# Reordering TensorE's first adaLN products and five late adaLN units in a two-layer convolution and attention trunk with mixture-of-experts

## The reference

```
m = silu(cvec) @ ada_w[i] + ada_b[i]          # (2 vectors) x 1024 x 6144, for each layer
h = rms_norm(x, g) * (1 + scale) + shift      # before the mixer and before the experts
y = y + gate * mixer(h);   y = y + gate2 * moe(h2)
q, k = rms_norm(q), rms_norm(k)               # layer 1; rotated for latent tokens
p = softmax([q @ k_local, q @ k_cached, sink])   # latent tokens; context tokens: own keys and sink
y_mixer = (p @ v) @ wo
```

## Time and profile before

| | us |
|---|---|
| median of three runs | 1288.72 |
| the profiled execution's own time | 1287.76 |
| its span, first to last instruction | 1285.9 |
| TensorE busy (share of span) | 1257.0 (98%) |
| VectorE busy | 442.9 (34%) |
| ScalarE busy | 327.5 (25%) |
| DMA, mean rate over the span | 387 GB/s |
| mean granted TensorE clock, share of full | 0.997 |

### The profile page before, as it was taken

One profiled execution on the slowest core, in us unless ns is written; L12 is line 12 of the kernel. 1 busy time (PEld: TensorE's weight loads), 2 busy tenths in 40 slices (PEclk: granted clock), 3 DMA queues, 4 the chain that ended last, 5 costly groups with the idle time before them and its releaser, 6 DMA issues.

```text
span 1285.9 us, 18888 instructions
## 1 busy us (share of the span) xinstructions
PE 1257.0 (98%) x6956; PEld 699.1 (54%) x6956; DVE 442.9 (34%) x1503; ACT 327.5 (25%) x728; POOL 62.3 (5%) x94
## 2 busy tenths in 40 slices
PE   7999999999999999999999899999999999999998
PEld 5776775544554455445454478554454445444544
DVE  3696372222222222222234727322222222222222
ACT  2486321221122112111131523222112212221211
POOL 0395000000000000000000000000000000000000
PEclk9999999999999999999999999999999999999999
DMA  9988999999999999999998786799999999999994
GB/s 331 382 335 365 406 395 397 417 419 419 421 421 419 420 421 421 421 420 420 392 382 346 173 359 229 304 407 419 419 420 421 421 420 421 421 420 420 420 418 194
DMA packets 87303, 497.43 MB, mean 387 GB/s; under 512 B 10889, under 2 KB 19761, under 8 KB 31952
## 3 DMA queue, kind: packets, MB, share of 16 engines
q1 hardware_dynamic: 86672, 496.47, 95.5%
q10 hardware_dynamic: 576, 0.22, 0.1%
HBM read 493.26 MB, written 3.41 MB: 386 GB/s over the span
## 4 chain that ended last, share of the span: by engine, by line
PE 86%; DVE 6%; DMA 4%; ACT 2%; issue 1%; POOL 0%; ACTq 0%; SPq 0%; DVEq 0%
PE ps L1024 33%; PE ps L1056 17%; PE ps L1067 9%; PE ps L995 7%; PE ps L661 4%; DMA S<-in_exp_w_up_dram 3%; DVE ps L1729 3%; PE ps L789 3%; PE ps L938 2%; PE ps L629 2%; PE ps L1042 1%; PE ps L979 1%; DMA W<-in_norm_ffn_dram 1%; PE ps L1034 1%; PE ps L649 1%
## 5 line engine op out<-in xcount | busy, mean ns | idle before, releaser
L1024 PE MATMUL ps<-ring,xg 128*64 128x512 f32 x1344 | 296.4, 593 | 0.2
L1024 PEld LDWEIGHTS ps<-ring,xg 128*64 128x64 f32 x1344 | 101.6, 137 | 189.4 <-issue 175.0
L1024 PE MATMUL ps<-S,xg 128*64 128x512 f32 x704 | 154.9, 592 | 1.2 <-DMA S<-in_exp_w_up_dram 1.2
L1056 PE MATMUL ps<-ring,W 128*64 128x512 f32 x672 | 153.5, 598 | 0.0
L2025 DVE TENSOR_TENSOR ypart<-ps,ypart 128x512 fp32r<-128x512 f32 x128 | 88.6, 692 | 179.8 <-ACT ypart L1514 179.8
L2014 DVE SCALAR_TENSOR_TENSOR vec<-silu_h,W,ps 128x256 f32<-128x256 f32 x64 | 30.8, 482 | 333.7 <-ACT silu_h L1508 333.6
L1067 PEld LDWEIGHTS ps<-comb,ypart 128*128 128x128 f32 x1024 | 126.3, 190 | 18.6 <-issue 18.6
L1067 PE MATMUL ps<-comb,ypart 128*128 128x256 f32 x1024 | 135.2, 285 | 0.0
L1508 ACT ACTIVATE silu_h<-ps 128x256 f32<-128x256 f32 x64 | 24.7, 386 | 408.2 <-PE ps L1024 408.2
L1503 ACT ACTIVATE xg<-ps 128x384 f32<-128x384 f32 x176 | 83.3, 492 | 168.0 <-PE ps L995 168.0
L1514 ACT ACTIVATE ypart<-ps 128x512 fp32r<-128x512 f32 x128 | 76.5, 597 | 184.6 <-PE ps L1056 184.6
(11 more groups left out here) (265 smaller groups left out, 1141.2 us busy)
## 6 DMA issues: line engine op xcount, KB each, us to landing
ring<-in_exp_w_gate_dram SPq DMA_DIRECT2D x86, 1024.0 KB, 16.1
ring<-in_exp_w_up_dram SPq DMA_DIRECT2D x86, 1024.0 KB, 19.4
ring<-in_exp_w_down_dram SPq DMA_DIRECT2D x86, 1024.0 KB, 19.2
S<-in_exp_w_gate_dram SPq DMA_DIRECT2D x44, 1024.0 KB, 16.8
S<-in_exp_w_up_dram SPq DMA_DIRECT2D x44, 1024.0 KB, 20.2
S<-in_exp_w_down_dram SPq DMA_DIRECT2D x44, 1024.0 KB, 19.3
ring<-in_ada_w_dram SPq DMA_DIRECT2D x24, 1024.0 KB, 20.5
S<-in_ada_w_dram SPq DMA_DIRECT2D x16, 1024.0 KB, 15.1
```

Of the source, the lines that this page charges most:

```text
L1024: mm = pe.matmul(PGU[64 * b:64 * b + 64, :].rearrange("p (h f) -> p h f", h=2), xg[:, places[k][m], 64 * b:64 * b + 64], gate_up_of(w[b])[ ...
L1056: mm = pe.matmul(bank[64 * b:64 * b + 64, :], hidT[:, j, 64 * b:64 * b + 64], down_of(w[b])[:, j, n * 512:(n + 1) * 512], start=(j == 0), ...
```

## The change: the order on TensorE, at two places

No other engine's list changes. The number of products that nobody reads rises by twelve; everything else is moved.

```diff
@@ front, in _(pe)
             pe.wait_ge(cond_ready, 1)
             sum_squares(1, 7)
+            keep_clock(ps[2], 20)
+            ada_half_products(0, 0)
             pe.wait_ge(ld_rows, 128)
             ... the ten transposes of the small rows
-            keep_clock(ps[2], 8)
-            for i in range(4):
+            for i in range(1, 4):
                 ada_half_products(0, i)
@@ heads of layer 1, in _(pe)
                     ada_products([EARLY + 10], ps[7])
                     at_values(0)
 
+                    ada_products([EARLY + 11], ps[7])
                     at_transposes(2)
                     at_scores(2)
-                    ada_products([EARLY + 11], ps[7])
                     at_transposes(3)
+                    ada_products([EARLY + 12], ps[7])
                     at_values(1)
 
                     at_transposes(4)
-                    ada_products([EARLY + 12], ps[7])
+                    ada_products([EARLY + 13], ps[7])
                     at_scores(3)
                     at_transposes(5)
-                    ada_products([EARLY + 13], ps[7])
+                    ada_products([EARLY + 14], ps[7])
                     at_values(2)
 
-                    ada_products([EARLY + 14], ps[7])
+                    ada_products([EARLY + 15], ps[7])
                     at_transposes(6)
-                    ada_products([EARLY + 15], ps[7])
                     at_transposes(7)
                     at_values(3)
```

## The result

The changed kernel takes 1290.85 us against 1287.42 us (medians of nine runs each, side by side): ratio 1.0028, interval 1.002 to 1.0037. It is 3.4 us slower. The forecast was +0.1, 1288.8 in all, and the range ended at 1290.8. (The three runs on which the forecast stands had a median of 1288.72, 1.3 us above that of the nine.) The profiled execution has a span of 1289.0 against 1285.9, +3.1 us, and the losses of this one execution can be read from it one by one.

A forecast was written before the change was run, and what follows sets the result against it. TensorE was taken as the bound, with the front waiting for unit 7's load and the heads for VectorE. Front 0.0, heads +0.1 and expert loads 0.0 gave +0.1 us, 1288.8 us; range 1286.5 to 1290.8.

The forecast's parts named there:

- The front's bound: Front: the last pair waits for unit 7's load at 24.2 us, so the new order gains nothing; term 0.0.
- Rival A: Front not bound by unit 7's landing: pair 3 at 21.8 instead of 25.2, -3.4 us; chance 0.07.
- the 3.7 us: Front: by the skill's clock rule, the stretch without its waits for loads would end 3.7 us earlier.
- The heads' order: Heads: filled waits come back as longer ones at `at_transposes(3)` and `at_transposes(7)`; term +0.1 us, bounds -0.2 and +0.4.
- the load of expert 0: Heads: the load would start at 726.7 instead of 730.56 us; term 0.0.
- Rival B: Heads pass on the filled waits before `at_transposes(2)` and `at_values(1)`: -1.8 us, 1287.0; chance 0.07.
- The clock: Front: two waits of 1.4 and 1.8 us replace one of 4.55; a clock fall at 24.3 would cost +1.3 to +5.0.
- rival C: Front: clock falls between 20 and 24.3 us, slowing the work behind: +1.3 to +5.0, 1290.1 to 1293.8; chance 0.13.
- C's long case: Front: half clock lasts through the first convolution chunk from 28.28, +5.0 us in all; chance 0.03.
- 1.9 us to spare: Front: the wait for unit 7 hides the twelve added products, which would otherwise cost 2.8 us.
- The page's rule: TensorE: a long pause between bursts of matmuls returns it to half rate; the trace agreed for the 4.55 us pause.

The follow-up runs named there:

- the repeat: The changed kernel measured again beside the kernel of before: 1290.57 against 1287.45 us, ratio 1.0025.
- heads part alone: Only the second half of the diff, the heads, applied to the kernel of before: 1289.88 against 1287.67 us, ratio 1.0015.
- the filler: Heads half of the diff on the kernel of before, plus 6 unread products ahead of the last head's transposes: 1287.55 against 1287.40 us, ratio 1.0002.
- front part alone: Only the first half of the diff, the front, applied to the kernel of before: 1288.28 against 1287.67 us, ratio 1.0006.
- its filler: Changed kernel plus 5 and 7 unread products in the front's two waits for loads: 1290.15 us against 1287.67 for before, ratio 1.0021.
- the kernel with both waits filled: Changed kernel plus 4 and 6 unread products in the front and 6 ahead of the last head's transposes: 1288.83 us against 1287.45 for before, ratio 1.0013.
- front part with eight products: Front half of the diff on the kernel of before, with 8 unread products instead of 20: 1288.48 against 1287.40 us, ratio 1.001.

## Why the prediction was wrong

- **The front's bound was right.** Pair 3 starts at 24.21 because unit 7 lands then, whatever TensorE did before; the waits were forecast at 1.4 and 1.8 us and measured at 1.30 and 1.64. Rival A is dead. One figure beside it, the 3.7 us by which the stretch without its waits would end earlier, has no working: rival A's own sum gives 3.4, and nothing else hangs on it.
- **The heads' order was right.** +0.1 forecast, +0.14 in the profile, and +0.15 in time once the wait is filled. The waits that are filled do come back one step later, and the load of expert 0 starts at 728.70, which less the 2.0 us is the 726.7 that was forecast. Rival B is dead.
- **The step that failed is "The clock".** It gave rival C 0.13 because "neither pause is nearly as long as the 4.55 us one", and it looked at the front alone. Pauses of 1.2 to 1.6 us were enough in three of five profiles with that front unfilled (once behind both, twice at the first), in the one place where the last pair and the transposes have no slack: +1.2 to +1.5, the size that C gave. The term for the heads was priced as a chain of engines, with the longer wait of 1.6 us "of idle time ahead of it in place of 0.57" written down and its clock not asked for. That was the larger loss: 1.3 and 0.35 in the profile, 3.0 in that of the repeat, +2.2 in the medians of the part alone. C's long case (half rate through the first chunk) did not occur in any profile, but its like did in the heads of the repeat.
- **A term was missing:** "1.9 us to spare" hides the twelve products' time but not their length in the list of instructions. They moved a fetch in front of the landing of a load that had 0.4 us of slack, 100 us later: +0.8 in the profile. How much of it reaches the medians is not shown.
- **The page's rule.** The Trainium skill ("TensorE: Matmul & The Clock Gate", section "Why this matters for your kernels") warns of a long pause. Here the clock fell at waits of 1.31, 1.54, 1.57 and 1.60 us, the first of them behind 7.5 us of work without a break, and in other executions it did not fall at such waits; the measurement decides. So the 4.55 us pause of before, which the prediction took as the measure, was no measure: with 1.54 us in its place the fall was the same.
- **The cost is not fixed.** My range treated the clock as one event, there or not. The same kernel took 1287.3 at a mean clock of 1.0 and 1293.4 at 0.993; the median depends on how often the falls come. The chance of C was too low: 0.13 for a fall that came in three of five profiles in the front alone.
- **What stays open:** the parts alone add up to 2.8 us (0.6 and 2.2) of the 3.1 to 3.4; that the clock is the cause is shown for the heads by the filler, and for the front by profiles only, since neither the front part (+0.6) nor its filler is clear of noise in the medians.

## What to carry to other kernels

Work that fills a wait does two things: it spends the time, and it keeps the matrix engine's clock up for what stands behind the wait. Before moving such work, list every wait that gets longer and ask what runs right behind it; a move that only exchanges waits can lose as much as a real delay. If it is moved all the same, a few unread products in the wait that is left can bring it back, as they did in the heads (+2.2 to +0.15 us), as long as they stay well inside the wait; in the front, where they took up all the slack, no gain is shown.

## What the runs showed of the hardware that was not expected

- The granted clock fell at the same instructions in one execution and not in another (front of the changed order: a fall in the profile of the changed kernel, none in that of the front part alone, with waits of 1.30 and 1.64 us in the one, 1.19 and 1.62 in the other). Nor is its length fixed: about 3.4 us in some profiles and 6.8 in others, at the same place (heads: 748.1 to 751.5 and 745.6 to 752.4). A single profile does not tell a kernel's cost at such a place, and the mean clock of many runs does so only in part: it went with the time in the repeat of the changed kernel (0.993 to 1.0, 1293.4 to 1287.3), but runs of before at 0.997 lie between 1285.9 and 1289.6, and the kernel with both waits filled has a higher median clock than before (0.998 against 0.997) and is 1.4 us slower.
- A fetch of TensorE's instructions keeps one of the 16 DMA engines for about 1 us (6.5% of 16 engines in a window of 1 us), and the 1 MB load of unit 23, when the fetch falls between its issue and its landing, lands 1.1 to 1.4 us later (9.7 against 10.8 to 11.1 us in seven profiles).
- The start of a launch scatters too: in two of the thirteen profiles (heads part alone, front part with eight products) TensorE waited 1.4 us more for the first rows of x. The first made it up before the chunk. In the second the loads landed 1.4 us later too, and with the fall of its clock it started the chunk at 31.04.
- The issue of a DMA can be held up by the ones before it: SP's seventh issue of an adaLN unit in the front took 6.84 us where the six before it took about 0.5 each, and ended at 12.2 us, 0.1 us after the first of them had landed (12.1; with eight products 13.9 and 13.8). That fits the full queue of which the prediction speaks, though the trace shows the times and not the queue.
